# The 512-column form of the gate and up products in a 14-sublayer float32 network on one core

## The reference

```
D_MODEL = 1024; SEQ = 256; D_FF = 2816

def rmsnorm(x, g, eps=NORM_EPS):
    xf = x.astype(jnp.float32)
    y = xf * lax.rsqrt(jnp.mean(xf * xf, axis=-1, keepdims=True) + eps)
    return (y * g.astype(jnp.float32)).astype(x.dtype)

def swiglu(x, w_in, w_out):                # x 256x1024, w_in 1024x5632, w_out 2816x1024
    gate, up = jnp.split(x @ w_in, 2, axis=-1)
    return (jax.nn.silu(gate) * up) @ w_out
```

## Time and profile before

| what | value |
| --- | --- |
| median of 3 runs | 3385.73 us (3384.61 to 3395.35) |
| profiled execution | 3391.96 us, span 3390.2 us |
| TensorE matmul busy | 3270.2 us, 96% of the span |
| VectorE busy | 1961.5 us, 58% |
| ScalarE busy | 1518.3 us, 45% |
| mean granted TensorE clock | 0.988 |
| HBM traffic | 153 GB/s over the span |

### The profile page before, as it was taken

How to read it: one execution, slowest core, us unless ns; L and a number is a source line. 1 busy time by engine, 2 the same in 40 slices (tenths; PEclk the granted TensorE clock), 3 DMA queues, 4 the chain that set the end, 5 groups by cost and what they waited for, 6 DMA issues and landing times.

```text
span 3390.2 us, 49870 instructions
## 1 busy us (share of the span) xinstructions
PE 3270.2 (96%) x21454; PEld 2885.9 (85%) x21454; DVE 1961.5 (58%) x2964; ACT 1518.3 (45%) x2539; POOL 175.0 (5%) x201
## 2 busy tenths in 40 slices
PE   7999999999999999999999999999999999999998
PEld 7987998987898987687989988987878888887897
DVE  4556556558556555574565565565456556825777
ACT  4455444455445443113444464454544344524554
POOL 0000000003000000230000000000011000100100
PEclk9998999999999999999999999999999999999999
DMA  7562656555656544314556554551013333531452
GB/s 252 187 198 88 220 191 226 190 170 166 206 190 225 187 151 157 125 45 155 187 181 224 187 165 166 190 168 28 26 63 112 123 123 129 179 93 63 136 187 100
DMA packets 413481, 522.06 MB, mean 154 GB/s; under 512 B 41639, under 2 KB 355740, under 8 KB 413132
## 3 DMA queue, kind: packets, MB, share of 16 engines
q1 hardware_dynamic: 407376, 515.92, 45.9%
q0 software_dynamic: 816, 2.10, 0.2%
q10 hardware_dynamic: 5068, 0.85, 0.1%
HBM read 516.21 MB, written 2.10 MB: 153 GB/s over the span
## 4 chain that ended last, share of the span: by engine, by line
PE 85%; DVE 8%; ACT 5%; issue 1%; POOL 0%; ACTq 0%; DMA 0%; DVEq 0%; POOLq 0%
PE ps L187 24%; PE ps L189 24%; PE ps L188 23%; PE ps L179 5%; PE ps L1332 2%; PE ps L197 2%; ACT a L1352 1%; DVE small L1389 1%; DVE a L1385 1%; ACT junk L723 1%; PE ps L869 1%; ACT a L1364 1%; PE ps L2044 1%; DVE fast_xt L776 1%; DVE tmp L706 1%
## 5 line engine op out<-in xcount | busy, mean ns | idle before, releaser
L187 PE MATMUL ps<-a 128*128 128x256 f32 (+1 forms) x4832 | 1513.3, 313 | 23.6 <-DVE fast_xt L776 8.4
L189 PE MATMUL ps<-a 128*128 128x256 f32 (+1 forms) x4664 | 1451.4, 311 | 0.0
L187 PEld LDWEIGHTS ps<-a 128*128 128x128 f32 x4832 | 909.6, 188 | 85.7 <-DVE a L1062 11.0
L188 PE MATMUL ps<-fast_xt,a 128*128 128x256 f32 x3400 | 953.8, 281 | 0.0
L189 PEld LDWEIGHTS ps<-a 128*128 128x128 f32 x4664 | 882.1, 189 | 52.4
L992 DVE TENSOR_TENSOR a<-ring,a 128x1024 fp32r<-128x1024 f32 x594 | 693.5, 1221 | 343.5 <-ACT a L986 343.5
L986 ACT ACTIVATE a<-ring 128x1024 fp32r<-128x1024 f32 x594 | 586.7, 1049 | 231.1 <-PE ps L189 231.1
L188 PEld LDWEIGHTS ps<-fast_xt,a 128*128 128x128 f32 x3400 | 640.2, 188 | 7.4
L188 PE MATMUL ps<-a 128*128 128x512 f32 (+1 forms) x1368 | 526.9, 385 | 0.0
L188 PEld LDWEIGHTS ps<-a 128*128 128x128 f32 x1368 | 257.3, 188 | 43.0
L1094 ACT ACTIVATE tmp<-ps 128x256 f32<-128x256 f32 x176 | 67.6, 384 | 478.9 <-PE ps L189 478.9
(11 more groups left out here) (380 smaller groups left out, 3938.9 us busy)
## 6 DMA issues: line engine op xcount, KB each, us to landing
ring<-in_ffn_w_in_dram SPq DMA_DIRECT2D x218, 1024.0 KB, 7.4
ring<-in_ffn_w_out_dram SPq DMA_DIRECT2D x121, 1024.0 KB, 5.0
ring<-in_ada_w_dram SPq DMA_DIRECT2D x48, 1024.0 KB, 5.3
ring<-in_swa_w_qkv_dram SPq DMA_DIRECT2D x12, 1024.0 KB, 7.7
ring<-in_gla_w_in_dram SPq DMA_DIRECT2D x12, 1024.0 KB, 7.4
ring<-in_rwkv_w_rkv_dram SPq DMA_DIRECT2D x12, 1024.0 KB, 5.1
ring<-in_na_w_qkv_dram SPq DMA_DIRECT2D x12, 1024.0 KB, 6.2
ring<-in_swa_w_o_dram SPq DMA_DIRECT2D x8, 1024.0 KB, 5.3
```

The lines of the kernel that those rows point to most:

```text
L187: pe.x.matmul(out, lh, rh, start=start and i == 0, stop=False)
L188: pe.x.matmul(out, lh, rl, start=False, stop=False)
L189: ins = pe.x.matmul(out, ll, rh, start=False, stop=stop and i == n - 1)
```

## The change

The high and the low input now lie side by side for each k (`x2`, 512 numbers: 256 high, 256 low), both in the arena. For each k the high weights are loaded once and take both through in one matmul of 512 columns: columns 0 to 255 receive high by high, columns 256 to 511 high by low. The low weights take only the high input through, 256 columns, added to columns 256 to 511. So a product has a whole PSUM bank and gate and up take two; two j are in flight instead of four. VectorE adds the two halves of a bank (`dve_sum`, a reduce over pairs of numbers that lie 256 apart) into SBUF, for gate and for up, and SiLU and the multiplication read those sums. In all FFNs from 1 on, the input is put 8 to 32 numbers further in the arena, and `ht` and `hs` are put off by 0 to 32 numbers more (`SPACE`). FFN 10 keeps the old form, with `ht` and `hs` 32 numbers further.

```diff
+def pe_up_both(K, pe, f, j):
+    s, x2 = K.s, K.ffn[f].x2
+    if j >= 2:
+        pe.wait_ge(*s.dve.at("sum", "u", f, j - 2))
+    for n, name in enumerate("gu"):
+        bank = K.ps[:, 2 * (j % 2) + n, :]
+        c, raw, wh, wl = piece_of(K, f, name, j)
+        pe.wait_ge(*s.dve.at("lo", name, f, j))
+        for k in range(8):
+            if j == 0 and k % 4 == 0:
+                for t in range(2):
+                    pe.wait_ge(*s.dve.at("xl", f, t, k // 4))
+            if k:
+                pe.x.matmul(bank[:, T:2 * T], wl[:, k, :], x2[:, k, 0:T], start=False, stop=False)
+            ins = pe.x.matmul(bank, wh[:, k, :], x2[:, k, :], start=k == 0, stop=k == 7)
+            if k == 0:
+                pe.x.matmul(bank[:, T:2 * T], wl[:, k, :], x2[:, k, 0:T], start=False, stop=False)
+        ins.then_inc(*s.pe.up("up", name, f, j))
...
 def act_silu(K, act, f, j):
     s = K.s
-    act.wait_ge(*s.pe.at("up", "u", f, j))
+    act.wait_ge(*s.dve.at("sum", "g", f, j))
...
-    act.x.activation(K.sg[j % 3], K.ps[:, j % 4, 0:T], AF.Silu).then_inc(*s.act.up("silu", f, j))
+    act.x.activation(K.sg[j % 3], K.gs[j % 2], AF.Silu).then_inc(*s.act.up("silu", f, j))
...
+def dve_sum(K, dve, f, j, name):
+    s, n = K.s, "gu".index(name)
+    bank = K.ps[:, 2 * (j % 2) + n, :]
+    dve.wait_ge(*s.pe.at("up", name, f, j))
+    dve.x.tensor_reduce((K.us if n else K.gs)[j % 2], bank.rearrange("p (two t) -> p t two", two=2), AX.X, ADD).then_inc(
+        *s.dve.up("sum", name, f, j))
...
 def dve_gate(K, dve, f, j):
     s = K.s
+    for name in "gu":
+        dve_sum(K, dve, f, j, name)
     dve.wait_ge(*s.act.at("silu", f, j))
-    dve.x.tensor_tensor(K.ffn[f].ht[j % 2], K.sg[j % 3], K.ps[:, j % 4, T:2 * T], MULT).then_inc(*s.dve.up("h", f, j))
+    dve.wait_ge(*s.dve.now())
+    dve.x.tensor_tensor(K.ffn[f].ht[j % 2], K.sg[j % 3], K.us[j % 2], MULT).then_inc(*s.dve.up("h", f, j))
...
+SPACE = {1: (8, 0), 2: (8, 8), 3: (16, 16), 4: (16, 32), 5: (32, 24), 6: (32, 8), 7: (24, 16), 10: (0, 32)}
```

More of the change, by code:

```diff
@@ L1022, in pe_down, with pe_up @@
             ins.then_inc(*s.pe.up("down half", f, t))
+def pe_up(K, pe, f, j):
+    s, (xh, xl) = K.s, K.ffn[f].xs
+    bank = K.ps[:, j % 4, :]
+    if j >= 4:
+        pe.wait_ge(*s.dve.at("h", f, j - 4))
+    for n, name in enumerate("gu"):
+        c, raw, wh, wl = piece_of(K, f, name, j)
+        pe.wait_ge(*s.dve.at("lo", name, f, j))
+        for half in range(2):
+            if j == 0:
+                for t in range(2):
+                    pe.wait_ge(*s.dve.at("xl", f, t, half))
+            ins = mm3(pe, bank[:, n * T:(n + 1) * T],
+                      [((wh[:, k, :], wl[:, k, :]), (xh[:, k, :], xl[:, k, :])) for k in range(4 * half, 4 * half + 4)],
+                      half == 0, half == 1)
+        ins.then_inc(*s.pe.up("up", name, f, j))
@@ L1025, in pe_core @@
 def pe_core(K, pe, f):
-    s, (xh, xl) = K.s, K.ffn[f].xs
+    up = pe_up if K.ffn[f].x2 is None else pe_up_both
     for j in range(NF):
[L1028 to L1041, removed]
+        up(K, pe, f, j)
@@ L4045, in small, with ffn_memory @@
     return a
-def ffn_memory(K, f, w_in, w_out):
+SPACE = {1: (8, 0), 2: (8, 8), 3: (16, 16), 4: (16, 32), 5: (32, 24), 6: (32, 8), 7: (24, 16), 10: (0, 32)}
+def ffn_memory(K, f, w_in, w_out, both=True):
     c = Core()
@@ L4051, in ffn_memory @@
     c.pieces = [(K.arena(1024, F32R), K.arena(1024, F32R)) for _ in range(6)]
-    c.xs = v3(K.arena(2048, F32R), T), v3(K.fast_xt[:, 0:2048], T)
-    K.arena(2048)
+    before_x, before_h = SPACE.get(f, (0, 0))
+    if before_x:
+        K.arena(before_x)
+    x = K.arena(4096, F32R)
+    if before_h:
+        K.arena(before_h)
+    c.x2 = v3(x, 2 * T) if both else None
+    c.xs = [c.x2[:, :, n * T:(n + 1) * T] for n in range(2)] if both else (v3(x[:, 0:2048], T), v3(K.fast_xt[:, 0:2048], T))
     c.ht = [K.arena(T) for _ in range(2)]
@@ L4117, in program @@
         K.sg = [K.tmp[:, 0, n * T:(n + 1) * T] for n in range(3)]
+        K.gs, K.us = [[K.tmp[:, 1, n * T:(n + 1) * T] for n in (i, i + 1)] for i in (0, 2)]
         with nc.sbuf_tensor("fast_gb", [128, 2 * D], F32R) as r:
@@ L4168, in program @@
         open_phase(K)
-        ffn_memory(K, 10, I["ffn_w_in_2"][1], I["ffn_w_out_2"][1])
+        ffn_memory(K, 10, I["ffn_w_in_2"][1], I["ffn_w_out_2"][1], False)
         M_conv = conv_memory(K, 10, 1, 0)
```

## The result

The changed kernel takes 3393.97 us (median of 20 runs, 3387.44 to 3401.79) against 3388.93 us before on the same chips: ratio 1.0017, interval 1.0009 to 1.0025. That is 5 us slower, inside the 0.3% that I had called no difference, and outside the range of the prediction by 2 us. I had forecast 11 us less.

A forecast was written before the change was run, and what follows sets the result against it. The prediction took PE's matmul slots to bound the kernel: 3391.96 (profiled) - 18.6 (up block) + 4.9 (down block) + 2.7 (FFN ends) = 3381.0 us, a median of 3375, range 3350 to 3392.

The forecast's parts named there:

- The bound: Inside an FFN the time is the sum of PE's slots; TensorE's matmuls are busy 96% of the span.
- E: VectorE becomes the bound through slow reduces: at 2.5 us each, 190 us slower, 3576; chance 0.05.
- The up pair: Up block: a 512- plus a 256-column slot takes 346.5 ns instead of 353.1 for three of 256, saving 18.6 us.
- adds to about the same as the steady slots: Where blocks meet, the first slots after a width change, 0.23 and 0.11 us, sum to about the steady ones.
- a 512-column slot after a 256-column one of over 232 ns: Up block: a sign, named in advance, that the forecast is wrong.
- The down block: From FFN 1 on, moved `hs` lengthens 2112 slots: 4.9 us lost, bounds 0 and 9.1 us.
- a half, 2.3 ns: Loss per down-block slot, taken as a half since nothing says all distances are bad; at most 4.3 ns.
- The ends: At each FFN's end SiLU drops out and the up sum comes in: +0.33 us, eight times, 2.7 us.
- The sum: Whole kernel: 3391.96 - 18.6 + 4.9 + 2.7 = 3381.0 us profiled; median 3374.7, stated as 3375.
- B: Distances eat the gain: up pair 351.0 ns, down slots 231.0 ns, +5.9 us in all, 3392; chance 0.25.
- D: Larger gain: new distances keep every up pair short, say 337 ns, saving 45 us, 3343; chance 0.13.
- C: Up block: a dropped matmul gives back only about a third of 7.9 ns, gaining 7 us; 3386; chance 0.07.

The follow-up runs named there:

- Grouped: The 512-column form at equal places, with each product's eight 512-column matmuls first and its eight 256-column ones after, instead of alternating: 3381.79 us, ratio 0.9971.
- the form alone: The changed kernel with no spaces (`SPACE = {}`), so input, pieces and gated pieces start at equal places: 3385.62 us, ratio 0.9987 against the kernel before.
- the fastest version: The 512-column form with `hs` at equal places, the input 160 bytes off and each FFN's last j in the old form: 3369.88 us, ratio 0.9945.

## Why the prediction was wrong

*The bound.* Right: PE's slots set the time inside an FFN, and neither the reduces (0.687 us against 0.69), nor the two banks, nor the new order on VectorE made PE wait there. E, the rival of VectorE as the bound, is out.

*The up pair: the larger of the two terms that were mis-sized.* I took 346.5 ns for a slot of 512 and one of 256 columns and got 349.3 at equal places (5.589 / 16), and 348.6 to 350.5 in the others. The up blocks gained 9.7 us and not 18.6, and with equal places everywhere it would have been 61 ns x 176 = 10.7. So 8 of the missing 9 us are the form's own. The step that failed is "adds to about the same as the steady slots". It rested on two single slots read to 10 ns, 0.23 and 0.11 us, to settle a term of 2 or 3 ns, and on the sum of two steady streams. Alternating is not that sum: in FFN 0 the slots of 512 columns behind one of 256 take 233.8 ns on average (226.7 steady), those of 256 columns 115.8 (120.0 steady). Grouped, the slots came back to 226 and 119. I had named this sign beforehand: a 512-column slot after a 256-column one of over 232 ns.

*The down block: the other term.* The step was "a half, 2.3 ns", with 4.3 ns as the most, for moved `hs`. Seven FFNs took 2.745 to 2.807 us where 2.730 stood, 0.427 us together, 9.4 us over 22 j, and FFN 10 1.6 more, its up block included: 11 us where I had 4.9 and a bound of 9.1. Per slot it is 1.3 to 6.4 ns. My bound came from the earlier trace rows, one stream with fewer stationary columns at distances that are not those of the change. Nearest is not near when the quantity goes up and down with the distance: 192 bytes costs 1.3 ns a slot, and 160 costs 5.3 in FFN 7 and 6.4 in FFN 6.

*The ends.* Right in mechanism and near in size: 3.1 us against 2.7, by the chain named, and it came back when the last j did without the reduce.

*The sum.* Forecast -18.6 + 4.9 + 2.7 = -11.0 us; by the rows -9.7 + 11.0 + 3.1 = +4.4 (the +4.2 of above, but for rounding). Two different things are in the miss. At equal places the form would still have come out 8.4 us faster, by the rows of the form alone; the distances took 11.3 us of it in the seven FFNs and 1.6 in FFN 10, and so turned the sign.

*The rivals.* B is what happened: the distances ate it. Its sum was +5.9 us with the ends, beside +5.0 measured, and I gave it 0.25. That the number is so near is partly luck: its pair of 351.0 was too long by 3.8 us in all and its down slots too short by 1.9, and it had no term for the alternation. D, that distances could be a gain, is right in direction only: the distance of 160 bytes gives 20 ns a j against equal places, 3.5 us, and no up block of any run comes below 5.558 / 16 = 347.4 ns a pair, where D had 337. The 19 us of the fastest version are mostly the form at equal places and the ends. C, little cost beside the columns, is out as a mechanism at like places, where a dropped matmul gave 164 / 16 = 10.3 ns in the up block alone and 11.7 over the whole j. In the number it did better than my forecast: against the kernel before, a dropped matmul gave back 3.4 ns on average over the eight FFNs, where C had 2.6 and I had 6.6, because two things changed at once. The Trainium skill (TensorE: Matmul & The Clock Gate, section Back-to-back issue gap) gives the 2.5 ns beside N / 2.4 for an isolated gap at the full clock. This stream of float32r matmuls, one weight load for each, is another case, and the 10.3 and 11.7 ns at like places do not agree with it.

I saw that slots depended on places and then treated it as a small correction between two bounds, while the change moved operands in eight ways and the form's whole gain was of the same size, 2% of a slot. And I priced an alternating stream from streams that don't alternate.

*What stays open.* Why the distance matters is not shown. That it is the distance between operands and repeats every 256 bytes is. Which pair counts, the weights that stream in under a matmul or those it uses, or one moving operand against the next, wasn't separated: in the old form, with the weights where they were, the place of the low input alone moved the up block by 103 ns. The low-input case and the blocks' borders show that more than one pair counts. That accesses of VectorE, ScalarE or the DMA engines to the same memory make the slots long was not tested. Against it stands that the pattern is TensorE's own: in the up block before, behind its first eight, the slots 113, 119, 117, 121, 117, 115, 120, 118 and 120 ns come round every nine matmuls, and they are the same from j to j within 2 ns.

## What to carry to other kernels

In this kernel a stream of float32r matmuls that each load weights has a slot that moves by up to 3% with where the operands lie against each other. Compare two forms only with the operands at like places, or with each form at its own best place; otherwise the layout is measured, not the form. Once a form is chosen, trying a few distances within 256 bytes in one run, one in each of several like stages, is cheap; take the best as it is measured, for it differs from form to form. Take it by the whole round of the loop, since one block's layout also moved the block behind it.

A stream that mixes two widths is not the sum of two steady streams. Here the mixture cost 2.6 ns a pair, 7 us of the 18.6 that I had hoped for.

An added step belongs where its chain is covered. The reduce was free in the loop and cost about 0.4 us only in the last round of each stage, where leaving it out brought it back.

## What the runs showed that I had not expected

- Slots of 512-column float32r matmuls with a weight load each took 227.0 ns in the down block (2.724 / 12) with `hs` at 0 or 256 bytes, 233 to 234 at most others, 228.8 at 192 (2.745 / 12).
- The time of a j goes in steps. In every FFN of every trace here, a j averaged over 16 j is a whole number of steps of 6.67 ns to within 0.1 ns: 8.380 us is 1257 steps, 8.313 is 1247, 8.293 is 1244. The steady slots fit too: 226.7 ns is 34 steps and 120.0 is 18. The distances move a j by whole steps, which suggests something in the stream that comes round every 6.67 ns; no run tests what it is.
- Moving all operands together by 32 bytes changed nothing, to the nanosecond; moving `hs` alone by 288 bytes, 32 beyond the period, made a down block 77 ns longer.
- The low input in the arena instead of in the fixed buffer: 26 us on 3390, with every instruction the same.
- Two forms of one product, alternating and grouped, have their best distances at 160 and 192 bytes, and each is poor at the other's.
